# Issue order of loads in the output stage of a hybrid decoder block, and the hand-over to its experts

## What is computed

```python
y = jnp.concatenate([oa, ob], axis=-1).astype(h.dtype)
return y @ w_out                      # then x += gate * out
...
h = rmsnorm(x) * (1 + scale) + shift
gp = softmax(h @ w_rg)                # 4 groups, the best one
el = softmax(h @ w_re)                # its 8 experts, the best two
...
hid = jax.nn.silu(xb @ w_gate[e]) * (xb @ w_up[e])
return hid @ w_down[e]                # x += gate * weighted sum of both experts
```

## Time and profile before

| | us |
|---|---|
| median of 3 runs | 2518.68 (2518.53 to 2520.19) |
| the profiled execution | 2507.53 |
| its span | 2505.4 |
| TensorE busy | 2206.2 (88%) |
| VectorE busy | 1126.5 (45%) |
| ScalarE busy | 922.0 (37%) |
| POOL busy | 382.8 (15%) |

### The profile page before, as it was taken

The page is one execution under the profiler, slowest core; times in us unless marked ns, Lnnn a source line. Parts: engine busy times, 40 slices in busy tenths (PEclk is TensorE's granted clock), DMA queues, the critical chain, the costliest instruction groups (busy, mean ns, idle before and its releaser), DMA issues. The chain is left out here.

```text
span 2505.4 us, 33260 instructions
## 1 busy us (share of the span) xinstructions
PE 2206.2 (88%) x9964; PEld 1242.9 (50%) x9965; DVE 1126.5 (45%) x2294; ACT 922.0 (37%) x2136; POOL 382.8 (15%) x320
## 2 busy tenths in 40 slices
PE   3999899999988897897999998878885998999990
PEld 2666544444444445896777774444552333333330
DVE  5444222232233752555888775656652222222223
ACT  1333111111233311224778774323323443444433
POOL 0000000000011101344333110010012222222220
PEclk9999999999999998998999999988887999999995
DMA  8444102211255544985223324343354988989747
GB/s 341 147 153 147 50 34 90 104 59 50 99 173 178 182 178 131 311 261 200 89 92 105 102 89 162 127 119 99 121 210 148 306 261 284 328 249 312 218 80 287
DMA packets 178320, 418.13 MB, mean 167 GB/s; under 512 B 41192, under 2 KB 81000, under 8 KB 162744
## 3 DMA queue, kind: packets, MB, share of 16 engines
q1 hardware_dynamic: 155944, 346.59, 39.6%
q0 software_dynamic: 13472, 45.26, 7.8%
q10 hardware_dynamic: 8816, 25.18, 2.9%
HBM read 296.84 MB, written 124.85 MB: 168 GB/s over the span
## 5 line engine op out<-in xcount | busy, mean ns | idle before, releaser
L644 PE MATMUL ps<-big,pc_w 128*128 128x512 f32 x1280 | 558.0, 597 | 10.6 <-DMA pc_w<-in_w_chan 10.6
L644 PEld LDWEIGHTS ps<-big,pc_w 128*128 128x128 f32 x1280 | 243.9, 192 | 312.3 <-issue 300.9
L2108 PE MATMUL ps<-big,ex_xt 128*64 x672 | 302.2, 603 | 2.1 <-ACT ex_xt L2151 2.1
L2109 PE MATMUL ps<-ex_wgu,ex_xt 128*64 128x512 f32 x672 | 302.2, 603 | 0.0
L1621 PE MATMUL ps<-w_out,mo_yt 128*128 128x512 f32 x512 | 235.5, 619 | 0.0
L309 PE MATMUL ps<-cp_wt,big 128*128 128x344 f32 x768 | 225.4, 454 | 0.0
L2159 ACT COPY ex_wgu<-big 128x4096 f32 x43 | 155.1, 3607 | 84.7 <-SPq L2025 51.9
L309 PEld LDWEIGHTS ps<-cp_wt,big 128*128 128x128 f32 x768 | 145.8, 191 | 76.9 <-issue 4.0
L1363 PE MATMUL ps<-at_v,at_pt 128*128 128x128 f32 (+1 forms) x1200 | 182.8, 290 | 0.0
L1429 ACT ACTIVATE at_p<-at_p,at_low 128x256 f32<-128x256 f32 (+1 forms) x384 | 174.0, 456 | 19.1 <-DVE at_low L1392 18.8
L2108 PEld LDWEIGHTS ps<-big,ex_xt 128*64 128x64 f32 x672 | 89.7, 139 | 181.1 <-issue 181.1
(11 more groups left out here) (295 smaller groups left out, 3187.8 us busy)
## 6 DMA issues: line engine op xcount, KB each, us to landing
big<-in_w_gate_up SPq DMA_DIRECT2D x32, 2048.0 KB, 11.2
ex_wd<-in_w_down SPq DMA_DIRECT2D x32, 1024.0 KB, 6.6
cp_w<-in_w_ada SPq DMA_DIRECT2D x24, 1024.0 KB, 5.4
ch_d<-pc_cv SPq DMA_DIRECT2D x20, 1024.0 KB, 4.1
at_v<-v_d SPq DMA_DIRECT2D x27, 512.0 KB
o_d<-at_o SPq DMA_DIRECT2D x48, 264.0 KB, 2.1
mo<-o_d SPq DMA_DIRECT2D x16, 792.0 KB
pc_qkv<-ch_d SPq DMA_DIRECT2D x16, 768.0 KB, 5.6
```

The lines of the kernel that those rows point to most:

```text
L644: last = nc.tensor.matmul(ps[:, n % 2, :], w[:, ch % 2, k, :], m.ht[:, k, g * BANK:(g + 1) * BANK], start=(k == 0), stop=(k == KD - 1))
L2108: nc.tensor.matmul(ps[0:HB, 2 + b, :], xt[:, b, k, 0:HB], wgu[:, bass.ds(at * WGU + k * 2 * DE, 2 * DE)], start=(k == 0), stop=(k == KD - 1))
L2109: last = nc.tensor.matmul(ps[HB:P, 2 + b, :], xt[:, b, k, HB:P], wgu2[:, b, k, :], start=(k == 0), stop=(k == KD - 1))
```

## The change

1. In the loop of SyncE's list in the output stage, `load_y` of tile t+2 is now called before `load_x` of tile t.
2. The down weights of experts 0 to 3 are loaded in the output stage, after its last output matmul (`w_done[1]`), into the memory of `w_out`, which the expert stage uses as its `wd`. The expert stage no longer loads or waits for them.
3. The first two gathers of tokens are issued by POOL at the end of the output stage, as soon as `slot_tok` is made (a new signal `slots_ready`), with their indices straight from `slot_tok` and into a part of `bias`. For that, `bias` and `w_out` are held to the end of the kernel, and buffers of the expert stage (`xt`, `sg`, `hid`, `hidt`) lie in `bias`.
4. The first copy into `wgu2` is made by VectorE instead of ScalarE, and the two first copies of indices are dropped.

The diff, cut to its core:

```diff
@@ mix_and_route, SyncE
                 with sp.Fori(0, NT // 2 - 2) as i:
                     for b in range(2):
+                        load_y(2 * i + (4 + b), b, i + 2)
                         load_x(2 * i + (2 + b), b, i + 1)
-                        load_y(2 * i + (4 + b), b, i + 2)
...
                 for e in range(NWB):
                     sp.dma_start(m.big[:, e * WGU:(e + 1) * WGU].rearrange("p (k n) -> p k n", k=KD), a["w_gate_up"][e]).then_inc(*first_in.inc)
+                sp.wait_ge(*w_done[1].n(PAIRS))
+                for e in range(NWB):
+                    sp.dma_start(m.wd[:, e * WD:(e + 1) * WD].rearrange("p (k n) -> p k n", k=DE // P), a["w_down"][e]).then_inc(*first_in.inc)
                 sp.wait_ge(*zero_out.n(2))
-                sp.wait_ge(*first_in.n(NWB))
+                sp.wait_ge(*first_in.n(2 * NWB))
@@ mix_and_route, POOL
                 pool.sem_inc(*lists_ready.inc)
+                for b in range(2):
+                    pool.wait_ge(*h_out[b].n(NT // 2))
+                pool.wait_ge(*zero_out.n(2))
+                pool.wait_ge(*slots_ready.n(1))
+                for b in range(2):
+                    pool.indirect_dma_start(out=m.xg[:, b, :], out_offset=None, in_=m.h_d.rearrange("t p n -> (t p) n"),
+                                            in_offset=bass.IndirectOffsetOnAxis(ap=m.slot_tok[:, b:b + 1].bitcast(U32), axis=0)).then_inc(m.xg_in[b], 16)
@@ mix_and_route, VectorE
-                link(V.tensor_tensor(m.slot_tok[:, :], fill[:, :], ps[:, 1, 0:P], ALU.add))
+                V.tensor_tensor(m.slot_tok[:, :], fill[:, :], ps[:, 1, 0:P], ALU.add).then_inc(*slots_ready.inc)
@@ experts
-        xg = R.sb("xg", [P, 2, D])
-        xt = R.sb("xt", [P, 2, KD, P])
+        xg = m.xg
+        xt = m.bias[:, 0:2 * D].rearrange("p (b k n) -> p b k n", b=2, k=KD)
...
-        wd = R.sb("wd", [P, NWB * (DE // P) * D])
+        wd = m.wd
@@ experts, SyncE
-                for b in range(NWB):
-                    load_down(b, b)
                 for b in range(NWB - 1):
-                    arrived(b, 0, 1)
+                    arrived(b, 0, 0)
@@ experts, POOL
                 pool.wait_ge(*zero_set.n(1))
-                gather(0, 0)
-                gather(1, 0)
@@ experts, ScalarE
-                copy_gate_up(0, 0)
                 take_x(0, 0, 0)
@@ experts, VectorE
-                take_idx(0, 0)
-                take_idx(1, 1)
+                started = dve.value_load(m.by_block[0:1, 0, 0:1], min_val=1, max_val=NE)
+                at = dve.value_load(m.by_block[0:1, 2, 0:1], min_val=0, max_val=NWB - 1)
+                dve.wait_ge(*gu_loaded.n(started))
+                dve.sem_inc(seen_dve, 1)
+                nc.vector.tensor_copy(wgu2[:, 0, :, :].rearrange("p k n -> p (k n)"), wgu[:, bass.ds(at * WGU, WGU)]).then_inc(*wgu2_ready[0].inc)
                 copy_down(0, 0)
@@ block_kernel
-        with nc.sbuf_tensor("bias", [P, NB * AH * 2 * P], F32) as m.bias:
...
+        m.bias = sb("bias", [P, NB * AH * 2 * P])
+        deltanet(nc, m, a)
+        m.w_out = ctx.enter_context(nc.sbuf_tensor("w_out", [P, KD, D], F32))
+        m.wd = m.w_out[:, :, :].rearrange("p k n -> p (k n)")
+        m.xg = m.bias[:, 4 * D:6 * D].rearrange("p (b n) -> p b n", b=2)
```

More of the change, by code:

```diff
@@ L55 @@
 WGU = KD * 2 * DE
+WD = DE // P * D
 def bucket_constants():
@@ L1983, in experts @@
         by = R.sb("by", [P, 2])
-        xg = R.sb("xg", [P, 2, D])
-        xt = R.sb("xt", [P, 2, KD, P])
+        xg = m.xg
+        xt = m.bias[:, 0:2 * D].rearrange("p (b k n) -> p b k n", b=2, k=KD)
+        sg, hid, hidt = (m.bias[:, 2 * D + n * 2 * DE:2 * D + (n + 1) * 2 * DE].rearrange("p (b n) -> p b n", b=2) for n in range(3))
+        hidt = hidt.rearrange("p b (k n) -> p b k n", k=DE // P)
         wgu = m.big
-        wd = R.sb("wd", [P, NWB * (DE // P) * D])
+        wd = m.wd
         wgu2 = R.sb("wgu2", [P, 2, KD, 2 * DE])
         wd2 = R.sb("wd2", [P, 2, DE // P, D])
-        sg = R.sb("sg", [P, 2, DE])
-        hid = R.sb("hid", [P, 2, DE])
-        hidt = R.sb("hidt", [P, 2, DE // P, P])
         y = m.mod[:, 0:2 * D].rearrange("p (b n) -> p b n", b=2)
@@ L2004, in experts @@
         added = R.sig("added")
+        R.sem_list.extend(m.xg_in)
         wgu2_ready, wd2_ready = S("wgu2_ready"), S("wd2_ready")
         gate = m.mod[:, 5 * D:6 * D]
-        WD = DE // P * D
         def blocks(eng):
@@ L2043, in _ @@
                         sp.dma_start(wgu[:, b * WGU:(b + 1) * WGU].rearrange("p (k n) -> p k n", k=KD), one(a["w_gate_up"], e)).then_inc(*wgu_in[b].inc)
-                        arrived((b - 1) % NWB, i + (1 if b else 0), i + (2 if b else 1))
+                        arrived((b - 1) % NWB, i + (1 if b else 0), i + (1 if b else 0))
                         sp.wait_ge(*y_done.n(free))
@@ L2047, in _ @@
                         load_down(e, b)
-                arrived(NWB - 1, NE // NWB - 1, NE // NWB)
+                arrived(NWB - 1, NE // NWB - 1, NE // NWB - 1)
             @block.gpsimd
@@ L2057, in gather @@
                     pool.sem_inc(seen, 1)
-                    pool.wait_ge(*idx_ready[b].n(q + 1))
+                    pool.wait_ge(*idx_ready[b].n(q))
                     pool.sem_inc(seen, 1)
@@ L2306, in block_kernel @@
         m.ps = ctx.enter_context(nc.psum_tensor("ps", [P, 8, BANK], F32))
+        m.xg_in = [nc.alloc_semaphore(name=f"xg_in{b}") for b in range(2)]
         m.ident, m.ones = m.cst[:, C_ID:C_ID + P], m.cst[:, C_ONE:C_ONE + P]
@@ L2323, in block_kernel @@
             phase(nc, m, a)
-        with nc.sbuf_tensor("bias", [P, NB * AH * 2 * P], F32) as m.bias:
-            deltanet(nc, m, a)
-            with ExitStack() as held:
-                m.w_out = held.enter_context(nc.sbuf_tensor("w_out", [P, KD, D], F32))
-                m.my = m.mod[:, 0:2 * D].rearrange("p (b n) -> p b n", b=2)
-                m.gain = held.enter_context(nc.sbuf_tensor("gain", [P, AW], F32))
-                m.wr = held.enter_context(nc.sbuf_tensor("wr", [P, KD, NG + NE], F32))
-                m.mo = held.enter_context(nc.sbuf_tensor("mo", [P, 2, NB, AW + 2 * AH], F32))
-                for phase in PHASES[3:5]:
-                    phase(nc, m, a)
+        m.bias = sb("bias", [P, NB * AH * 2 * P])
[3 more added lines that the diff above has]
+        m.xg = m.bias[:, 4 * D:6 * D].rearrange("p (b n) -> p b n", b=2)
+        with ExitStack() as held:
+            m.my = m.mod[:, 0:2 * D].rearrange("p (b n) -> p b n", b=2)
+            m.gain = held.enter_context(nc.sbuf_tensor("gain", [P, AW], F32))
+            m.wr = held.enter_context(nc.sbuf_tensor("wr", [P, KD, NG + NE], F32))
+            m.mo = held.enter_context(nc.sbuf_tensor("mo", [P, 2, NB, AW + 2 * AH], F32))
+            for phase in PHASES[3:5]:
+                phase(nc, m, a)
         for phase in PHASES[5:]:
```

4 lines of the change are left out of this document (2 added, 2 removed).

## The result

| | before | changed |
|---|---|---|
| median | 2518.61 us (4 runs, 2513.36 to 2520.19) | 2449.91 us (4 runs, 2448.05 to 2451.12) |
| ratio | | 0.9729, interval 0.9715 to 0.9744 |
| profiled execution | 2507.53 | 2450.97 |
| its span | 2505.4 | 2448.7 |
| first matmul of tile 2's output to that of tile 14 | 269.12 | 208.87 |

The kernel is 68.7 us faster. The forecast was 2454 with a range of 2445 to 2478, so the time fell inside, 4 us under the point. The stages of the table show that the term of the loop came out 3.6 us larger than forecast and that the term of the hand-over nearly failed.

The account below looks back on a forecast made before the run. The prediction took the output stage as loosest, held by a loop of waits around late attention rows. Terms of -56.7 (loop) and -8.2 (hand-over) sum to -64.9, from 2518.7 to 2454 us, range 2445 to 2478.

Parts of the forecast that it names:

- the term of the loop: Output stage: rows issued earlier end VectorE's waits, twelve steps at 17.7 us take 212.4 instead of 269.1: -56.7 us.
- the term of the hand-over: From slot_tok to the experts: early gathers and VectorE's copy bring the first expert matmul to 1902.8 instead of 1911.0: -8.2 us.
- The down weights: Four 1 MB loads moved behind the last output matmul: cost nothing, hidden by the routing tail with 21 us to spare.
- The feared 4 us on POOL's scatters: Routing tail: early down weights may lengthen POOL's four list scatters per pair of tiles by 4 us; taken as 0.
- The landing: Early 512 KB gather at the hand-over: 3 to 4 us to land, before the barrier lets go; bounds 2.5 and 8.1.
- VectorE's copy: Start of expert stage: first gate weights' copy takes 2.46 us, behind the memset (0.9) and two register loads (0.5).
- The carried 11 us: Whole kernel: the unprofiled median's 11 us above the profiled execution were added unchanged to the forecast.
- The rivals: Four alternatives: rows landing late 0.07, VectorE or ScalarE bounding 0.08, swap not advancing rows 0.03, x late 0.02.
- The rows were punctual: Rival in the output loop: rows land much later, beside ScalarE's stores; at 22 us landing 2485 us; chance 0.07.
- VectorE has 9.8 of 47 us idle: Rival in the output loop: VectorE or ScalarE becomes the bound, six steps lose 18 us in all, 2472; chance 0.08.
- x lands as before: Rival in the output loop: x becomes the late load; at 35 us landing 2539 us, slower than before; chance 0.02.

Follow-up runs that it names:

- e2: Only the swap of load_y and load_x, in the kernel before: 2452.34 us, ratio 0.9742.
- e3: The changed kernel without the swap, x issued first again: 2516.1 us, ratio 1.0003.
- e1: The kernel before, no edit, for a second trace: 2514.02 us.
- e4: Kernel before, but SyncE, after waiting for x's two conditions, issues y and the attention rows ahead of x: 2500.93 us, ratio 0.9943.
- e12: Against e11, the first four experts' down weights are loaded in the expert stage again, behind the gathers: one execution, 2439.76 us.
- e9: Changed kernel, but each of the two early gathers brings only 64 columns (32 KB instead of 512 KB): one execution, 2451.96 us.
- e8: Changed kernel with one early gather, the second issued at the start of the expert stage: 2449.4 us, ratio 0.9723.
- e6: Changed kernel, but POOL issues both first gathers inside the expert stage, straight from slot_tok: 2449.2 us, ratio 0.9708.
- e11: The edit of e6 again, five rounds beside the unchanged changed kernel: 2446.94 us, ratio 0.9701.
- e7: Changed kernel, but POOL waits for both gathers to land before ending its output-stage list: 2450.25 us, ratio 0.9721.
- e10: The changed kernel unchanged, in the same rounds and on the same chip as e11: 2450.36 us, ratio 0.9709.

## Why the prediction was right, and where it was not

**The swap: right, the size 3.6 us short.** The term was -56.7 us, from twelve steps at 17.7; the trace gives -60.25. I had put the six odd steps at 17.7 where the calculation itself offered 17.2 for them (-59.7), and 17.2 is what they take, and one even step with them. The rest of the working held: rows had 9.5 to 11.6 us to land, the pass shown had 10.0, and VectorE did not wait; SyncE's x goes out 9.4 us behind the rows (forecast: some 9); the granted clock is 1.0. The cause is shown by three runs: the swap alone has the whole loop time of the change (e2), everything else without it has that of before (e3, 274.8 beside e1's 275.0), and the rows ahead of x but behind its waits get only 14 us (e4). I had seen the slow transposes behind the idling (1.97 us instead of 1.04) but not priced them: that a third of the lost time was TensorE's slow work came into the sum only because I compared with a step without both.

**The down weights: right, nothing.** From tile 14's block to `slot_tok` it is 70.17 before and 70.18 after, with 4 MB more on the queues. The feared 4 us on POOL's scatters did not come, and e12 shows that moving them had no effect on the first matmul either, once the gathers are first.

**The gathers: wrong, -1.8 instead of -8.2.** The step that failed is "The block then starts at 1896.5 + 2.38 = 1898.9": I took VectorE's idle time of 2.38 us at the barrier of before and hung it behind POOL's last issue. But that was time spent waiting for POOL's DRAIN, in which POOL had nothing outstanding. In the changed kernel the DRAIN lasts 7.95 us, and the block opens 7.4 us behind POOL's last issue, because the end of the stage waits for the gathers to land (e9: 3.0 us less when they land 2.9 sooner; e8: 2.5 less with one instead of two; e6, e11 and e12: 2.7 us as before with none). Of the 6.4 us that this term was off, 5.7 lie here, between `slot_tok` and the opening of the block (10.41 instead of 4.73). So all engines stood and waited for data that only TensorE needed. A smaller part of the same step: POOL's first issue comes 0.83 us after `slot_tok`, I had allowed 0.1. The landing was priced too low as well, 3 to 4 us where each of the two took 5.4. By itself that would have cost 0.1 us: issued at 1894.3, the first gather is there at 1899.7, and 3.2 us later the transposes' branch ends at 1902.9, beside the 1902.8 of the copy's branch. By the Trainium skill (DMA: Bandwidth & Descriptors, Anatomy of one DMA) one gather would take 3.2 us, an estimate from its fit. The traces show more: 4.4 from the issue of a gather to the transposes that wait for it, with a second one behind it (e11), and for one that moves alone (e8) 3.9 from the issue to the end of its last packet.

**VectorE's copy: right in size and on the path, its surroundings 0.8 us short.** It took 2.39 us (forecast 2.46), and as forecast it is the last thing that the first matmul waits for. But it starts 1.10 us behind the memset, where I had allowed 0.5 for two register loads, and the matmul follows 0.25 us behind it. So from the opening to the first matmul it is 4.66 us instead of 3.9. What moving the copy to VectorE is worth by itself is not shown, since no run moved it alone.

**The carried 11 us: only half right.** I carried the distance between the profiled execution and the median over unchanged. e1's execution was 6.5 us longer than the profiled one, and 5.9 of it lay in the output loop, where the swap removes the waits. With the swap the loop time is 208.87 us in the traces of the changed kernel, e2, e7, e8, e11 and e12, and 209.2 to 210.1 in those of e6, e9 and e10. So a part of the 11 us vanished with the loop's waits, and the changed kernel's profiled execution lies 1 us from its median. In the sum the errors stand so, trace against trace: 4.5 us later at tile 2's block (in code that the change does not touch), -3.6 from the swap, +6.4 from the hand-over, +0.8 behind it. That is 8.1 of the 8.4 us by which the profiled execution lies above its forecast of 2442.6; and in the median they are more than paid for by the 11 us that did not come. That the point was only 4 us off is luck: errors of opposite sign met, and the terms themselves were less good.

**The rivals.** None took over. The rows were punctual, VectorE has 9.8 of 47 us idle, and x lands as before in the median (4.5 us beside 4.6) though the longest now takes 9.2 instead of 4.9, with two steps of cover:

```profile
DMA to landing us min/median/max: 3.8/4.5/9.2
```

## What to carry to other kernels

In a queue that executes in order, ask of each load which wait stands ahead of it that it does not need itself; here a load held up by another's wait closed a loop through four engines, and two swapped lines were worth 2.6%. When such waits go, count the slow work that follows each of them too: a third of the gain was TensorE back at its full clock. And a transfer issued ahead of a barrier of all engines starts earlier but can make everybody wait for it; issuing it first behind the barrier, ahead of the large loads, gave an earlier first matmul in the traces (10.7 to 10.8 us behind `slot_tok` instead of 14.8 to 15.1) with less code.

## What was not expected of the hardware

- The end of a stage waits for the landing of gathers that POOL has issued in it. POOL's DRAIN at the end of its list lasted 2.83 us with nothing outstanding (`before`, e6), 5.94 with one gather of 512 KB (e8) and 7.95 with two. From the last packet to the next stage's first instruction it is 3.2 us in the traces of the changed kernel, e3, e8, e9 and e10. In e7, where POOL waits for the landing itself, it is 4.9: a DRAIN of 3.0 us still follows the wait. Loads that SyncE issued were not tested for this, since its list waits for them anyway.
- A 512 KB gather issued 2.2 us ahead of 4 MB of loads took 4.44 us to its consumer, the same as without them, and no packet of the loads moved before it had landed; issued 0.2 us behind them, 9.0, of which 4.5 passed before its first packet moved.
- POOL needed 0.82 to 0.83 us from the end of `slot_tok` to its issue, in each of the six traces in which it waited for it.
